# Attention on one core: another order of TensorE's work within a step, and weighted values one unit later

## What is computed

```python
DILATION_PATTERNS = ((128, 1), (512, 4), (2048, 16))       # three groups g, 16 heads of 64 each
qkv = (x @ w_in).reshape(b, s, 3, N_GROUPS, 16, 64)
for g, (window, dilation) in enumerate(DILATION_PATTERNS):
    q = rms_norm(qkv[:, :, 0, g], q_gain[g]) * 64 ** -0.5
    k = rms_norm(qkv[:, :, 1, g], k_gain[g])
    # causal windowed attention with a bias: scores, max, exp, sum, weighted values
    o, l = dilated_window_attention(q, k, qkv[:, :, 2, g], rel_bias[:, g], window, dilation)
wts = softmax(stack(lses), axis=0)                          # merge the three groups
y = einsum('gbsh,gbshe->bshe', wts, stack(outs)) @ w_out
```

## Time and profile before

| | |
|---|---|
| median of 3 executions | 3436.91 us |
| profiled execution, first to last instruction (span) | 3436.1 us |
| granted TensorE clock, mean | 0.966 of full |
| PE busy over the span | 3198.9 us, 93% |
| 61 to 1305 us (attention): length, PE / DVE / ACT busy | 1244.00, 1201.57 / 656.11 / 663.15 us |

### The profile page before, as it was taken

How to read it: one execution, slowest core, us unless ns; L and a number is a source line. 1 busy time by engine, 2 the same in 40 slices (tenths; PEclk the granted TensorE clock), 3 DMA queues, 4 the chain that set the end, 5 groups by cost and what they waited for, 6 DMA issues and landing times. The chain is left out here.

```text
span 3436.1 us, 48994 instructions
## 1 busy us (share of the span) xinstructions
PE 3198.9 (93%) x17450; PEld 2676.8 (78%) x17450; DVE 1280.0 (37%) x3617; ACT 1186.2 (35%) x3147; POOL 862.0 (25%) x622
## 2 busy tenths in 40 slices
PE   5999999999999994899999999799877799999999
PEld 3888888888888873678888888578756588888887
DVE  6445554555545553341212122631163521212121
ACT  4555555555455552231212122320243321213130
POOL 3333333333233310132222212212111222222221
PEclk9999999999999995999999999899998899999999
DMA  2112121121112114111111110111201111111111
GB/s 96 38 37 61 40 57 51 50 53 45 52 43 60 38 27 166 37 43 49 47 49 46 49 49 31 42 39 49 86 27 60 37 49 49 50 50 49 49 43 68
DMA packets 88749, 177.48 MB, mean 52 GB/s; under 512 B 25259, under 2 KB 55614, under 8 KB 88510
## 3 DMA queue, kind: packets, MB, share of 16 engines
q1 hardware_dynamic: 88510, 174.35, 16.1%
HBM read 161.19 MB, written 13.12 MB: 51 GB/s over the span
## 5 line engine op out<-in xcount | busy, mean ns | idle before, releaser
L1092 POOL TENSOR_TENSOR mlp_w_lo<-mlp_raw,mlp_w_hi 128x1024 fp32r<-128x1024 f32 x128 | 306.3, 2393 | 1094.7 <-ACT mlp_w_hi L1054 1094.7
L69 PE MATMUL ps_qk<-w_hi,attn_hT_hi 128*128 128x256 f32 x1536 | 439.3, 286 | 23.1 <-DVE attn_hT_lo L213 9.7
L71 PE MATMUL ps_qk<-w_hi,attn_hT_lo 128*128 128x256 f32 x1536 | 437.9, 285 | 0.0
L70 PE MATMUL ps_qk<-w_lo,attn_hT_hi 128*128 128x256 f32 x1536 | 437.7, 285 | 0.0
L69 PE MATMUL mlp_ps<-mlp_hT_hi,mlp_w_hi 128*128 128x512 f32 x1024 | 406.0, 396 | 26.0 <-DVE mlp_hT_lo L213 20.9
L70 PE MATMUL mlp_ps<-mlp_hT_lo,mlp_w_hi 128*128 128x512 f32 x1024 | 402.2, 393 | 0.0
L71 PE MATMUL mlp_ps<-mlp_hT_hi,mlp_w_lo 128*128 128x512 f32 x1024 | 401.8, 392 | 0.0
L69 PE MATMUL mlp_ps<-mlp_hid_hi,mlp_w_hi 128*128 128x512 f32 x1024 | 398.3, 389 | 0.0
L70 PE MATMUL mlp_ps<-mlp_hid_lo,mlp_w_hi 128*128 128x512 f32 x1024 | 398.3, 389 | 0.0
L71 PE MATMUL mlp_ps<-mlp_hid_hi,mlp_w_lo 128*128 128x512 f32 x1024 | 398.3, 389 | 0.0
L857 POOL TENSOR_TENSOR w_lo<-raw,w_hi 128x384 fp32r<-128x384 f32 x192 | 194.9, 1016 | 701.7 <-ACT w_hi L602 701.7
(11 more groups left out here) (292 smaller groups left out, 6400.4 us busy)
## 6 DMA issues: line engine op xcount, KB each, us to landing
mlp_raw<-in_w SPq DMA_DIRECT2D x128, 512.0 KB, 3.4
raw<-in_wqkv SPq DMA_DIRECT2D x192, 192.0 KB, 2.3
w_bc<-share_dram SPq DMA_DIRECT2D x48, 256.0 KB, 4.1
mi_raw<-in_vo_pieces SPq DMA_DIRECT2D x16, 512.0 KB, 3.4
bias<-bias_dram SPq DMA_DIRECT2D x16, 256.0 KB, 3.5
yT_dram<-o_g SPq DMA_DIRECT2D x8, 512.0 KB, 3.0
attn_out_raw<-in_attn_wo SPq DMA_DIRECT2D x8, 512.0 KB, 5.0
attn_out_y_raw<-yT_dram SPq DMA_DIRECT2D x8, 512.0 KB, 4.1
```

The costliest lines, as they stand in the source:

```text
L69: pe.matmul(out, a_hi, b_hi, start=first, stop=False)
L70: pe.matmul(out, a_hi, b_lo, start=False, stop=False)
L71: return pe.matmul(out, a_lo, b_hi, start=False, stop=last)
L1092: pool.tensor_tensor(w_lo[:, q % 2].rearrange("p k c -> p (k c)"), raw[:, q % RAW_SLOTS, :], w_hi[:, q % 2].rearrange("p k c -> p (k c)"). ...
```

## The change

Only PE's program in the attention phase changes. The blocks of a step become functions and are called in another order, and O works on the unit of two steps ago, not of one. The other engines' programs are the same, instruction for instruction.

```diff
+                def weighted_values():
                     if has_unit(st, j, 2):
+
+                        sec, u = unit(st, j, 2)
+                        g = sec % NG
+                        whole = TT * sec + u
                         pe.wait_ge(p_hi_done, U - 1)
                         pe.wait_ge(p_lo_done, U - 1)
-                if has_unit(st, j, 1):
-                    sec, u = unit(st, j, 1)
-                    pe.wait_ge(p_hi_done, U)
-                    pe.wait_ge(p_lo_done, U)
-                    if has_unit(st, j, 2):
-                        pe.wait_ge(o_done, U - 1)
+                        if has_unit(st, j, 3):
+                            pe.wait_ge(o_done, U - 2)
...
+                query_key_tile()
+                weighted_values()
+                if j == 0:
+                    turn_tiles()
+                value_part()
+                scores()
+                if j != 0:
+                    turn_tiles()
+                turn_probabilities()
```

More of the change, by code:

```diff
@@ L503, in step @@
                 par = st % 2
[L504 to L510, removed]
-                        if j == 0:
[L512 to L535, removed]
@@ L536, in step, with query_key_tile @@
-                if has_unit(st, j, 1):
-                    sec, u = unit(st, j, 1)
-                    g = sec % NG
-                    pe.wait_ge(exp_done, U)
+                def query_key_tile():
+                    if st < SECTIONS:
+                        if st >= 1 or j >= 2:
+                            pe.wait_ge(qkn_done, T - 1)
+                        for k in range(KT):
+                            if st == 0 and j % 4 == 0:
+                                norm.wait_tile(pe, j // 4, k)
+                            if j == 0:
+                                pe.wait_ge(w_hi_done, TT * N + k + 1)
+                                pe.wait_ge(w_lo_done, TT * N + k + 1)
+                            mm = split_matmul(pe, ps_qk[j % 2][:, 0:2 * P],
+                                              hT_hi[:, k, j * P:(j + 1) * P], hT_lo[:, k, j * P:(j + 1) * P],
+                                              w_hi[:, par, k, 0:2 * P], w_lo[:, par, k, 0:2 * P], k == 0, k == KT - 1)
+                        mm.then_inc(qk_mm, 1)
@@ new lines, in turn_tiles @@
+                def turn_tiles():
+                    if (st >= 1 or j >= 1) and st <= SECTIONS:
+                        if TT * st + j >= 2:
+                            pe.wait_ge(turn_hi, T - 1)
+                            pe.wait_ge(turn_lo, T - 1)
+                        if TT * st + j - 1 < TT * SECTIONS:
+                            pe.wait_ge(qkn_done, T)
+                            for a in range(2):
+                                mm = pe.transpose(ps_t[:, a * P:(a + 1) * P], qkn[:, (j - 1) % 2, a * P:(a + 1) * P], ident[:])
+                        if st >= 1:
+                            if j == 0:
+                                pe.wait_ge(vT_done, 2 * N)
+                            mm = pe.transpose(ps_t[:, 2 * P:3 * P], vT[:, (st - 1) % 2, j * P:(j + 1) * P], ident[:])
+                        if j == 1 and st >= 2 and (st - 2) % NG < 2:
+                            pe.wait_ge(exp_done, U - 1)
+                            pe.wait_ge(neg_done, U - 1)
+                            mm = pe.transpose(ps_t[0:4 * TT, 3 * P:4 * P], stat[:, (st - 2) % 2, :], ident[:])
+                        mm.then_inc(turned, 1)
@@ new lines, in turn_probabilities @@
+                def turn_probabilities():
+                    if has_unit(st, j, 1):
+                        sec, u = unit(st, j, 1)
+                        g = sec % NG
+                        pe.wait_ge(exp_done, U)
+                        if has_unit(st, j, 2):
+                            pe.wait_ge(p_hi_done, U - 1)
+                            pe.wait_ge(p_lo_done, U - 1)
+                        for h in range(2):
+                            for b in range(0 if has_prev(g, u) else 1, 2):
+                                c = (2 * b + h) * P
+                                mm = pe.transpose(ps_p[:, c:c + P], prob[:, u % 2, h, b * P:(b + 1) * P], ident[:])
+                        mm.then_inc(p_turned, 1)
@@ new lines, in value_part @@
+                def value_part():
+                    if st < SECTIONS:
+                        half = j // 4
+                        if j == 0 and st >= 1:
+                            pe.wait_ge(vT_done, 2 * N)
+                        if j == 4:
+                            pe.wait_ge(vT_done, 2 * N + 1)
+                        for k in range(2 * (j % 4), 2 * (j % 4) + 2):
+                            mm = split_matmul(pe, ps_v[:], w_hi[:, par, k, 2 * P:3 * P], w_lo[:, par, k, 2 * P:3 * P],
+                                              hT_hi[:, k, half * HALF:(half + 1) * HALF],
+                                              hT_lo[:, k, half * HALF:(half + 1) * HALF], k == 0, k == KT - 1)
+                        if j % 4 == 3:
+                            mm.then_inc(v_mm, 1)
@@ new lines, in scores @@
+                def scores():
+                    if has_unit(st, j, 0):
+                        sec, u = unit(st, j, 0)
+                        g, sp_ = sec % NG, sec % 2
+                        if j == 0:
+                            pe.wait_ge(turn_hi, T)
+                            pe.wait_ge(turn_lo, T)
+                        if has_unit(st, j, 1):
+                            pe.wait_ge(exp_done, U)
+                        k0 = (u - 1) * P if has_prev(g, u) else u * P
+                        c0 = 0 if has_prev(g, u) else P
+                        for h in range(2):
+                            rows = slice(HD * h, HD * h + HD)
+                            mm = split_matmul(pe, ps_s[h][:, c0:2 * P],
+                                              qk_hi[rows, sp_, 0, u * P:(u + 1) * P], qk_lo[rows, sp_, 0, u * P:(u + 1) * P],
+                                              qk_hi[rows, sp_, 1, k0:(u + 1) * P], qk_lo[rows, sp_, 1, k0:(u + 1) * P],
+                                              True, True)
+                        mm.then_inc(scored, 1)
@@ new lines, in weighted_values @@
+                        first = 0 if has_prev(g, u) else 1
+                        for b in range(first, 2):
+                            slot = (whole - 1 + b) % 3
+                            mm = split_matmul(pe, ps_o[:, 0:2 * P], v_hi[:, slot, :], v_lo[:, slot, :],
+                                              pT_hi[:, b, :], pT_lo[:, b, :], b == first, b == 1)
+                        mm.then_inc(pv_done, 1)
+                query_key_tile()
+                weighted_values()
+                if j == 0:
+                    turn_tiles()
```

## The result

The changed kernel takes 3536.27 us (median of 4), the kernel before, timed beside it, 3438.03: a ratio of 1.029, 95% interval 1.0275 to 1.0305. It is 98 us slower. The forecast was 3570 with 3500 to 3612 around it. The spans of the profiled executions, 3436.1 and 3534.9 us, differ by 98.8, and all of it lies in the attention phase: the first matmul of the output projection starts 98.2 us later (1434.1 for 1335.9), and what follows takes the same time to less than 1 us.

What follows compares the result with a forecast made beforehand. PE, busy 93% of the span, was taken to bound the kernel. To 3436.1 us came 75 at full clock, 58 for clock falls and 0.8 to the median: 3570 us, range 3500 to 3612.

Steps and rivals of the forecast that it cites:

- (b): Inside sections: the circle of waits runs through S, T, P; ordinary steps unchanged, delayed ones wait at S, +2.45 us per pair.
- (c): At j = 0: S also needs T's evacuation, behind ScalarE's other work; idle 8.05 us against 1.2, +6.85 per pair.
- The rival on the faster side: P's old stall goes and nothing replaces it, if the maximum needn't follow T and P's evacuation: 3392 to 3415 us, 4%.
- (a): P at the step's end, behind S, never waits again; before, this cost about 3.5 us per pair of heads.
- (d): O two steps back never waits; ScalarE's copies of `ps_o` wait for O behind QK, hidden in ordinary steps and borders.
- the drain: Steps behind the last section, without QK or V to hide anything: about 1 us more each for eight and a bit, +9.
- The sum at full clock: Attention phase: seven pairs 65 us, first sections' borders +4.5, last section's end +9, loop turns −4; together +75 us.
- The seams: Tiling-mode switches around S: entering from V and leaving to T pay the same as before; 0 taken, −21 us or the opposite open.
- The clock: QK after the longer new idle times runs at half clock: 24 falls of 2.4 us each, 58 us.
- the hole that the prediction had between 1.4 and 2.8 us: No profile row showed an idle time of such length, so the clock's cost lay between 19 and 94 us; 58 taken.

Runs made afterwards that it cites:

- max_early: Changed kernel's PE order, with VectorE taking bias and maximum of the scores in the same step, ahead of evacuating P and T: 3439.04 us, ratio 1.0003 to the kernel before.

## Why the prediction was right, and where its sizes were off

- **The direction and the mechanism, (b) and (c), held.** S waits for the exponentials inside sections and for `v_lo` at j = 0. In sum the waits of S inside sections and at j = 0 were to be 5.95 and 8.05 us per pair of heads; in sections 7, 8 and 9 together the trace has 0.24 + 0.45 + 1.24 + 2.04 + 0.35 + 1.76 + 0.34 = 6.4 and 2.25 + 3.71 + 2.70 = 8.66. The rival on the faster side fell: the maximum does have to follow the evacuation, until *max_early* takes it out.
- **(a)** P's waits went, as forecast (24 us; 25 in PE's starts, 19 of them P's own and the rest O's behind them).
- **(d)** The lag was to be hidden, and is in the ordinary steps of the changed order. That it costs 20 us where T and P follow O directly was not foreseen. That O never waits failed in the drain, where O has no QK ahead of it: nine waits for `pT_hi`, 9.2 us.
- **The sum at full clock**, 75 us, came out as 73: 73 of waits (104.6 − 31.7; the forecast had 65 + 4.5 − 4 = 65.5), 12.5 of drain (forecast 9), −9 in the table's last row, where 0 was taken and −21 to +21 left open, and −3 in sections 0 and 1, which the prediction does not have. That the total agrees to 2 us is luck: 7 us more of waits and 3.5 more of drain made up for what the seams and the first sections gave back.
- **The seams.** An ordinary narrow step is 0.07 us shorter, and this is the sum of four differences: O behind QK takes 0.35 us where it took 0.47 behind S, T behind S takes 0.05 more than behind QK (0.38 for 0.33), and V no longer pays the 0.08 of the block behind P (1.48 for 1.56), which QK now pays (2.95 for 2.87). "TensorEngine Tiling (Array Packing)", Key Properties, in the Trainium skill says that a change of tiling mode drains TensorE. A cost that is the same whatever follows would have left the step as it was; here leaving S cost O 0.12 us and costs T 0.05.
- **The clock** is the term that was mis-sized: 24 falls of 2.4 us each were forecast, 58 us; QK lost 28.9 us after against 4.6 before, 24 us. Eighteen QKs beside those at the two loop turns were slow. The number of falls was forecast a little high, the price of one far more so. It had been read from a loop turn, where QK met nothing but half clock. Behind a wait of S the clock was at half for a shorter time. The window over the QK that follows the wide border, from its start to that of O:

```profile
472.53:476.98 4.45, 4.45 (x28) 4.45 (x26) 1.72 (x8) 1.39 (x5) 0.00 (x0) 0.62 0.42 122
```

4.45 us for 2.95: 1.5 lost, not 2.4. With that price the forecast would have been 3570 − 24 x 0.9 = 3548, and with 18 of them 3539; 3536 was measured. After the idle 3.55 us at the border the clock was at 1.2 GHz for part of QK and then at 2.4 again.

## What to carry over

When a block of one engine is moved behind another, look for the order written on the *other* engines: here ScalarE and VectorE still evacuated the transposes before they turned to the scores, so moving the transposes behind the scores joined two chains that had run side by side. A change of one engine's order is worth judging only together with the order of those that serve it: the same PE program was 2.9% slower, equal, or 1.0% faster, as the maximum and the evacuation at the border were placed. And the free time of a circle of waits is what decides the price of everything in it: the small merge instructions cost a step 0.5 us before and 1.24 after, the 1.2 us ones nothing and 0.35.

## What was not expected

- Waits of the same length did not always cost the clock. Leaving out loop turns, the QK after S's wait at j = 0 was slow in 6 of 6 cases at 3.7 us, in 5 of 6 at 2.72 and in 3 of 4 at 2.25 (groups 2 to 0). It was slow after 2.03 us in section 22, but not after 2.36, 2.50 and 2.95 us in sections 2, 3 and 23. Inside sections the QK after 1.77 us was slow in 3 of 7 cases, and after 2.05 us in none of 7. Most of these waits lie in the hole that the prediction had between 1.4 and 2.8 us, but their length alone does not decide; what decides a single case no run here tells.
- The drain of the last section, where the circle has no projections to hide behind, went from 45.0 to 57.5 us, and to 49.8 with the earlier maximum.
